# Another form of the RWKV inverse, of the head sums and of the S5 transposes, with other beat counts, in a three-layer hybrid kernel

## Chip, cores and metric

The kernel runs on one core of a Trainium2 chip. The metric is the device time of one execution in microseconds (us); less is better.

## What is computed

A sequence of 256 tokens of width 2048 passes two layers of a first block and one layer of a second, all in float32.

```python
# first block, layers l = 0, 1
shift, scale, gate = split(silu(c) @ w_ada[l] + b_ada[l], 3)
h = rms_norm(x, norm_g[l]) * (1 + scale) + shift
u, z_s, q, k, v, z_a = split(h @ w_in[l])            # 6144 columns
y_s = s5_mixer(u, ...) * silu(z_s)                   # 64 groups, 64 complex states each, then w_glu
y_a = diff_attention(rope(q), rope(k), v, ...) * silu(z_a)      # 8 heads
x = x + gate * (concat(y_s, y_a) @ w_out[l])
# second block, one layer
z_rw, z_mla, z_gate = split(rms_norm(x) @ w_in_2)
def step(state, r, w, k, v, kk, a):                  # rwkv7_scan, 16 heads of 64
    sa = state @ -kk
    state = state * w + sa (x) (kk * a) + v (x) k
    return state, state @ r
mix = (g_rw * (y_rw @ w_branch_rw) + g_mla * (y_mla @ w_branch_mla)) @ w_out_2
# then an up/conv/gelu/down feed-forward and a gated embedding, each with its norm
```

## The kernel before, in words

All activations lie transposed: channels on partitions, the 256 tokens along the free axis. The big products run as one stream through TensorE (PE). A weight tile of 128 output channels is a row of 16 (or 8, 4, 22) blocks of 128 rows; for each block `mm` multiplies a high and a low part of the float32 weights with a high and a low part of the activation, three matmuls of 256 columns. The weights come by DMA in half units of eight blocks into a ring; ScalarE (ACT) writes the high part (`hi`), VectorE (DVE) the low part (`lo`), each 128x1024. `split_ahead` and `rest` place these two beats in the order of the work.

**The order is written out beforehand.** `Timeline` makes one list of beats; each of the five engine programs walks over it and plays its own part of each beat, so every engine's queue follows this one order. Small work is woven into the stream by generators. Each step of a generator ends with a number of `yield`s, which is the number of beats until its next step. With `per=2`, as in most of `w_in`, one beat of the generators comes after two blocks (six matmuls). The counts stand in the tables `S5_PREP`, `S5_RUN`, `S5_PHASE`, `ATTENTION`, `RWKV` and `MOD_REST`, the first four with a row for each of the two layers.

**The start.** `modulation` multiplies `w_ada`, 1 MB a unit. When the last quarter of the scale is there, `gp` and four `h` (the normed activations, high part by ACT, low by DVE) follow, and then `w_in` starts. Before them stands

```python
                if parts == 3:
                    self.split_ahead(1)
                    self.rest(0)
```

which puts the first two `hi` and the first `lo` ahead of the last four `h`. The later modulation units are woven into the stream; `MOD_REST` holds the beats between the request for a unit and its matmuls, for `w_in`'s first eight tiles, for the rest of `w_in` with `w_outa`, and for the last two streams.

**S5.** 16 blocks of four groups per layer. `s5_prepare` makes the matrices of block b+1 while `s5_follow` runs block b; a block ends when the longer one has ended (`s5_phases` too in every second block). In the preparation the taps are multiplied in step 6 (PE), copied by ACT in step 7, written by GpSimd (POOL) to the DRAM scratch `scr_k`, and read back in step 8 by four DMAs into `WI`, with overlapping rows. In the run, step 0 makes the inputs `x` in bank 3, step 1 (ACT) copies them to `XT`, twice side by side, step 2 (PE) transposes `XT` and `XT` shifted by 64 columns, so that DVE has real and imaginary halves in both orders, step 3 (DVE) rotates and scans, step 4 (PE) waits for `WI` and for the scan and makes `y`.

**RWKV.** Eight pairs of heads `i` in chunks of 32 tokens; a pair is steps 0 to 14 of `rw`. Step 0 multiplies the low-rank weights `LW` (`GD2`, `GD` for the gate into bank 5, two halves for decay and `a` into banks 3 and 4, then `over` for the key norms). Its signal `d` lets ACT, DVE and again PE (`rk`, step 3) go on. Step 4 makes the score blocks, and DVE masks them. Sixteen 32x32 blocks (two heads, two token halves, four chunks) form a strictly triangular matrix whose inverse is needed. With the 16x16 blocks on the diagonal, steps 6 to 9 build the inverse `EE` by squaring; steps 10 and 11 add the corner part: `OT` times `EE` and a transposed `EE`, ACT copies, `ET` times `TO`, which DVE adds to `EE`; step 12 applies `EE` to `Q0T` (`apply`, 96 columns) and ACT copies the result to `QTT`. Step 13 makes `G` and the transition matrices, step 14 the chunk sums in banks 3 to 6 for states (64 columns) and for outputs (32 columns), which DVE takes out as `Af` and `Y` (signal `af`, which step 0 of the next pair waits for).

**`rw_seq`.** Steps c = 1 to 7 run over the chunks for all 16 heads: PE makes the carried states (`tf`) and output parts (`ty`), heads of one parity on partitions 0 to 63 and the others on 64 to 127 of one bank; DVE scales, adds, and adds the outputs to `Y`. Two beats of stream lie behind each step. DVE's queue holds `cq` and `part` work between them.

Of the kernel before, what the change touches and what calls it, by code (L numbers as in the profile page):

```python
# [26 lines left out]
for _n, _c in PARAMS:  # L27
# [4 lines left out]
    ("ident", 128), ("rot", 128), ("ones", 128), ("blk", 128), ("spare", 256), ("caus", 128), ("chk", 128),  # L32
    ("m16s", 32), ("m32i", 32), ("m16t", 32), ("m32t", 32), ("mot", 32), ("i32", 32), ("scm", 256), ("id64", 64),
# [14 lines left out]
def const_array():  # L48
# [75 lines left out]
ROOM = _c.alloc(320)  # L124
# [50 lines left out]
OT, ET, TO = (BTM + 128 * n for n in range(3))  # L175
# [99 lines left out]
def kind_of(name, n):  # L275
# [44 lines left out]
class Timeline:  # L320
# [429 lines left out]
    def run(self):  # L750
# [15 lines left out]
        for n, _ in enumerate(first):  # L766
# [323 lines left out]
def tensor_program(pe, m, tl, D):  # L1090
# [111 lines left out]
    def s5_run(l, b, i):  # L1202
# [67 lines left out]
    def rw(i, s, slot):  # L1270
# [34 lines left out]
        if s == 0:  # L1305
# [17 lines left out]
        if s == 4:  # L1323
# [3 lines left out]
            if i:  # L1327
                pe.wait_ge("rw_dve", ("af", i - 1))
# [48 lines left out]
        if s == 13:  # L1377
            pe.wait_ge("rw_act", ("a3", i))
# [3 lines left out]
        if s == 14:  # L1382
            pe.wait_ge("rw_dve", ("vm", i))
            rows(0, 64, KE, 64, VTK, 64)
            rows(256, 32, VTK, 64, MRK, 32).then_inc("rw_pe", ("e", i))

    def rw_seq(c):
# [3 lines left out]
        if c < 7:  # L1391
            for i in range(8):
                for hd, p in enumerate(rows):
                    x = pe.mm(B(3, 64 * i, 64, **p), V(BK + 512 * i + 64 * c, 64, **p), V(before + 64 * i, 64, **p), True, True)
            x.then_inc("rw_pe", ("tf", c))
        pe.wait_ge("rw_dve", ("ys", c - 1))
        for i in range(8):
            for hd, p in enumerate(rows):
                x = pe.mm(B(5, 32 * i, 32, **p), V(before + 64 * i, 64, **p), V(G + 256 * i + 32 * c, 32, **p), True, True)
# [111 lines left out]
def scalar_program(act, m, tl, D):  # L1511
# [1419 lines left out]
```

## Time and profile before

| what | value |
|---|---|
| median of three runs | 2895.5 us (2895.36 to 2900.58) |
| profiled execution, own time | 2895.5 us |
| its span | 2893.6 us |
| PE busy | 2781.8 us (96%) |
| DVE busy | 2008.9 us (69%) |
| ACT busy | 1468.2 us (51%) |
| POOL busy | 288.5 us (10%) |
| chain that ended last | PE 84%, DVE 7%, DMA 6% |

The profile is of one execution. The span runs from the first to the last instruction; the own time holds what lies around it, 1.9 us. Busy times are sums over an engine's instructions. The chain that ended last goes back from the last instruction to what released it, step by step.

### The profile page before, as it was taken

How to read it: one execution, taken by the hardware profiler on the slowest of the kernel's cores; microseconds unless marked ns; L12 is line 12 of the kernel's file. 1: busy time of each engine (PE TensorE's matmuls, PEld its weight loads, DVE VectorE, ACT ScalarE, POOL GpSimd, SP SyncE). 2: the span in 40 equal slices, each digit the busy share in tenths (PEclk: the TensorE clock that was granted, in tenths of full speed). 3: DMA queues.
4: the chain of work that ended last, by engine and by line, in shares of the span. 5: the costliest groups of instructions: out<-in, count | busy, mean ns of one | idle time of the engine just before them, and what ended most of it. 6: DMA issues, size and time to landing. Idle time of an engine off the chain costs nothing.

```text
span 2893.6 us, 64415 instructions
## 1 busy us (share of the span) xinstructions
PE 2781.8 (96%) x27664; PEld 2593.9 (90%) x27664; DVE 2008.9 (69%) x3478; ACT 1468.2 (51%) x2406; POOL 288.5 (10%) x488
## 2 busy tenths in 40 slices
PE   6899999999999999999999999999999999999987
PEld 2678788788999999999889889999999999999987
DVE  6357778687799986765556566666888547887565
ACT  3335556355566656644444435456555445555454
POOL 0012222100123221200011011100000000000000
PEclk9899999999999999999999999999999999999999
DMA  9988788885756566555444445554555555555543
GB/s 392 332 267 269 260 287 267 292 310 169 205 171 199 175 204 197 181 175 169 140 144 150 140 133 170 180 193 161 185 182 187 184 184 180 181 185 187 182 153 110
DMA packets 168236, 581.08 MB, mean 201 GB/s; under 512 B 40272, under 2 KB 40304, under 8 KB 155536
## 3 DMA queue, kind: packets, MB, share of 16 engines
q1 hardware_dynamic: 146784, 525.40, 54.2%
q0 software_dynamic: 20592, 48.26, 5.4%
q8 instruction: 218, 3.57, 0.5%
q10 hardware_dynamic: 576, 3.31, 0.3%
q14 instruction: 66, 0.54, 0.1%
HBM read 555.06 MB, written 21.76 MB: 199 GB/s over the span
## 4 chain that ended last, share of the span: by engine, by line
PE 84%; DVE 7%; DMA 6%; ACT 1%; issue 1%; SPq 1%; POOL 0%; DVEq 0%; ACTq 0%
PE acc L1011 82%; DMA arena<-in_w_ada 3%; DVE arena L979 2%; PE acc L1014 2%; DVE rounded L979 2%; DMA scr_k<-arena 1%; DMA arena<-scr_k 1%; SPq L976 1%; DVE upper L987 1%; DMA scr_u<-upper 0%; DVE arena L987 0%; ACT arena L1008 0%; DVE rounded L987 0%; DVE upper L979 0%; DMA arena<-in_w_outm 0%
## 5 line engine op out<-in xcount | busy, mean ns | idle before, releaser
L1011 PE MATMUL acc<-rounded 128*128 128x256 f32 x14592 | 1861.9, 286 | 18.6 <-issue 10.1
L1011 PEld LDWEIGHTS acc<-rounded 128*128 128x128 f32 x14592 | 1783.5, 192 | 86.2 <-issue 61.2
L1008 ACT ACTIVATE rounded<-arena 128x1024 fp32r<-128x1024 f32 (+1 forms) x862 | 875.3, 1022 | 694.5 <-PE acc L1011 583.5
L979 DVE TENSOR_TENSOR rounded<-arena,rounded 128x1024 fp32r<-128x1024 f32 (+1 forms) x830 | 983.9, 1198 | 246.7 <-ACT rounded L1008 246.1
L1011 PEld LDWEIGHTS acc<-upper_rounded,rounded 128*128 128x128 f32 x4656 | 560.8, 192 | 18.2 <-issue 9.8
L1011 PE MATMUL acc<-upper_rounded,rounded 128*128 128x256 f32 x4656 | 567.7, 284 | 2.8 <-DVE rounded L979 2.0
L1008 ACT ACTIVATE arena<-arena 128x256 f32<-128x256 f32 (+3 forms) x473 | 232.9, 515 | 170.8 <-DVE arena L979 105.4
L979 DVE TENSOR_TENSOR arena<-acc,arena 128x256 f32<-128x256 f32 (+5 forms) x270 | 113.7, 431 | 233.7 <-PE acc L1011 221.0
L979 DVE TENSOR_TENSOR arena<-arena 128x256 f32<-128x256 f32 (+5 forms) x455 | 233.3, 526 | 35.9 <-ACT arena L1008 27.5
L987 DVE SCALAR_TENSOR_TENSOR arena<-arena 128x256 f32<-128x256 f32 (+5 forms) x465 | 205.1, 446 | 27.7 <-ACT arena L1008 19.6
L1011 PE MATMUL acc<-arena 128*32 128x512 f32 (+6 forms) x1990 | 183.2, 402 | 41.7 <-DMA arena<-in_w_ada 27.6
L1008 ACT ACTIVATE arena<-acc 128x256 f32<-128x256 f32 (+3 forms) x267 | 99.2, 384 | 187.6 <-PE acc L1011 179.2
L1011 PEld LDWEIGHTS acc<-arena 128*32 128x32 f32 (+2 forms) x1990 | 69.6, 123 | 97.0 <-DMA arena<-in_w_ada 50.7
L1008 ACT ACTIVATE upper<-acc 128x128 f32<-128x128 f32 (+3 forms) x184 | 67.4, 380 | 114.2 <-PE acc L1011 82.5
L1008 ACT ACTIVATE arena<-acc,arena 128x256 f32<-128x256 f32 (+1 forms) x148 | 59.3, 428 | 103.3 <-PE acc L1011 91.2
L1011 PE MATMUL acc<-upper 32*32 32x32 f32 (+8 forms) x4384 | 101.3, 218 | 9.1 <-issue 3.3
L1011 PEld LDWEIGHTS acc<-upper 32*32 32x32 f32 (+4 forms) x4384 | 73.1, 114 | 30.0 <-issue 13.5
L976 POOL DMA_DIRECT2D arena<-scr_k x128 | 77.3, 621 | 122.5 <-DMA scr_k<-arena 121.8
L1011 PE MATMUL acc<-upper,arena 64*64 64x64 f32 (+4 forms) x490 | 63.0, 350 | 13.7 <-DMA upper<-in_w_ada 6.9
L976 POOL DMA_DIRECT2D scr_g<-arena x56 | 30.4, 545 | 440.4 <-DVE arena L990 236.6
L1014 PE MATMUL acc<-arena 128*128 128x128 f32 x416 | 71.2, 276 | 2.8 <-ACT arena L1008 2.3
L1008 ACT ACT_TABLE_LOAD x56 | 71.8, 1283 | 4.0 <-issue 3.0
(92 smaller groups left out, 1116.0 us busy)
## 6 DMA issues: line engine op xcount, KB each, us to landing
arena<-in_w_in SPq DMA_DIRECT2D x328, 512.0 KB, 4.8
arena<-in_w_ada SPq DMA_DIRECT2D x88, 1024.0 KB, 5.5
arena<-in_w_up SPq DMA_DIRECT2D x176, 512.0 KB, 3.9
arena<-in_w_down SPq DMA_DIRECT2D x88, 512.0 KB, 4.2
arena<-in_w_outa SPq DMA_DIRECT2D x32, 512.0 KB, 6.0
arena<-in_w_glu SPq DMA_DIRECT2D x32, 512.0 KB, 5.8
arena<-in_w_outm SPq DMA_DIRECT2D x32, 512.0 KB, 4.6
arena<-in_w_out SPq DMA_DIRECT2D x32, 512.0 KB, 3.8
```

Of the source, the lines that this page charges most:

```text
L976: self.e.dma_start(out, in_).then_inc(self.signals.sems[sem], 16)
L979: return self.put(self.e and self.e.tensor_tensor(o, a, b, op))
L987: return self.put(self.e and self.e.scalar_tensor_tensor(out=o, in0=a, scalar=s, in1=b, op0=o1, op1=o2))
L1008: return self.put(self.e and self.e.activation(o, a, f, scale=scale, **kw))
L1011: return self.put(self.e and self.e.matmul(o, l, r, start=start, stop=stop, skip_group_check=True))
L1014: return self.put(self.e and self.e.transpose(o, i, self.m.con("ident")))
```

## The change

- The beats `split_ahead(1)` and `rest(0)` ahead of the last four `h` are taken out; the splits follow behind them.
- The beat counts of S5, of attention and of `MOD_REST` are others.
- S5, run: ACT copies 128 columns to `XT` instead of 256. PE transposes them once, and makes the second, swapped order by two matmuls of 64 stationary columns each with the identity.
- RWKV steps 10 to 12: instead of completing `EE` and applying it once, `EE` is applied to `Q0T`, the corner part `OO` (masked by DVE in step 4 from the other scores) to the result, and `EE` again to that; DVE adds the first and the last. ACT copies 384 columns after steps 10 and 11.
- RWKV step 14: the outputs come from four matmuls over all 128 partitions with 128 columns; DVE spreads `MRK` with the chunk mask to `MRW` for it (128x512, in step 13). They lie in bank 7, and ACT copies them to `Y`.
- RWKV step 0: `kr` is waited for first and `gd` last; the two halves for `d` come first, `over` next, the gate last, with 32 rows of `GD2` instead of 64.
- `rw_seq`: the heads of the two parities go to two banks (3 and 4, 5 and 6), and DVE does its product and its sum out of them in two instructions of 64 partitions.
- The constants lose 128 columns, and `ROOM`, which nothing uses, gains them.

```diff
-S5_PREP = ((0, 0, 3, 7, 1, 5, 0, 3, 0),
-    (0, 2, 0, 4, 2, 6, 2, 2, 0))
-S5_RUN = ((1, 3, 1, 7, 1, 3, 1, 2),
-    (1, 5, 2, 6, 1, 3, 1, 1))
-S5_PHASE = ((18, 1),
+S5_PREP = ((0, 1, 3, 6, 1, 6, 1, 2, 0),
+    (1, 2, 2, 4, 3, 3, 3, 1, 0))
+S5_RUN = ((1, 3, 1, 6, 2, 3, 2, 1),
+    (1, 4, 3, 6, 2, 1, 1, 1))
+S5_PHASE = ((13, 5),
     (17, 2))
 S5_START = (6, 8)
-ATTENTION = ((1, 1, 3, 2, 3, 4, 4, 1, 2, 1, 1, 2, 5, 2, 1),
-    (1, 1, 2, 2, 1, 1, 4, 1, 5, 2, 3, 3, 3, 1, 2))
+ATTENTION = ((1, 2, 4, 2, 3, 2, 4, 1, 3, 1, 1, 2, 2, 2, 1),
+    (1, 1, 2, 1, 2, 2, 4, 1, 5, 2, 2, 3, 3, 2, 1))
 RWKV = (1, 3, 3, 6, 3, 4, 2, 2, 2, 1, 2, 2, 2, 4, 1)
-MOD_REST = (2, 3, 2)
+MOD_REST = (2, 2, 2)
...
-                if parts == 3:
-                    self.split_ahead(1)
-                    self.rest(0)
...
             pe.wait_ge("s5_act", ("xt", l, b))
+            pe.tr(B(3, 256, 128), V(XT, 128))
             for h in range(2):
-                x = pe.tr(B(3, 256 + 128 * h, 128), V(XT + 64 * h, 128))
+                x = pe.mm(B(3, 384, 128, p0=64 * h, np_=64), V(XT + 64 - 64 * h, 64), con("ident"), True, True)
...
+            pe.wait_ge("rw_dve", "kr")
+            pe.mm(B(3, 0, 256), V(LW, 128, np_=64), V(LO, 256, np_=64), True, True)
+            pe.mm(B(4, 0, 256), V(LW, 128, p0=64, np_=64), V(LO, 256, p0=64, np_=64), True, True).then_inc("rw_pe", ("d", i))
+            over(6, 0, KNR + 2 * i).then_inc("rw_pe", ("kk", i))
             pe.wait_ge("rw_dve", "gd")
-            pe.mm(B(5, 0, 256), V(LW + 256, 128, np_=64), V(GD2, 256, np_=64), True, False)
-            pe.mm(B(4, 0, 256), V(LW, 128, p0=64, np_=64), V(LO, 256, p0=64, np_=64), True, True)
-            pe.mm(B(3, 0, 256), V(LW, 128, np_=64), V(LO, 256, np_=64), True, True).then_inc("rw_pe", ("d", i))
-            pe.mm(B(5, 0, 256), V(LW + 128, 128), V(GD, 256), False, True).then_inc("rw_pe", ("g", i))
-            pe.wait_ge("rw_dve", "kr")
-            over(6, 0, KNR + 2 * i).then_inc("rw_pe", ("kk", i))
+            pe.mm(B(5, 0, 256), V(LW + 128, 128), V(GD, 256), True, False)
+            pe.mm(B(5, 0, 256), V(LW + 256, 128, np_=32), V(GD2, 256, np_=32), False, True).then_inc("rw_pe", ("g", i))
...
         if s == 10:
             pe.wait_ge("rw_dve", ("e3", i))
-            four(3, OT, EE)
-            for u, p in chunks():
-                x = pe.mm(B(4, 32 * u, 32, **p), V(EE + 32 * u, 32, **p), V(CON + CCOL["i32"], 32, **p), True, True)
-            x.then_inc("rw_pe", ("a1", i))
+            apply(3, EE, 32, Q0T).then_inc("rw_pe", ("a1", i))
         if s == 11:
             pe.wait_ge("rw_act", ("a1", i))
-            four(5, ET, TO).then_inc("rw_pe", ("a2", i))
+            apply(5, OO, 32, QTT).then_inc("rw_pe", ("a2", i))
         if s == 12:
-            pe.wait_ge("rw_dve", ("a2", i))
+            pe.wait_ge("rw_act", ("a2", i))
             apply(3, EE, 32, Q0T).then_inc("rw_pe", ("a3", i))
...
-            rows(0, 64, KE, 64, VTK, 64)
-            rows(256, 32, VTK, 64, MRK, 32).then_inc("rw_pe", ("e", i))
+            rows(0, 64, KE, 64, VTK, 64).then_inc("rw_pe", ("e", i))
+            for u, (hd, hf) in enumerate(U4):
+                x = pe.mm(B(7, 128 * hf, 128, p0=64 * hd, np_=64), V(VTK + 64 * u, 64), V(MRW + 128 * u, 128), True, True)
+            x.then_inc("rw_pe", ("y", i))
...
-                    x = pe.mm(B(3, 64 * i, 64, **p), V(BK + 512 * i + 64 * c, 64, **p), V(before + 64 * i, 64, **p), True, True)
+                    x = pe.mm(B(3 + hd, 64 * i, 64, **p), V(BK + 512 * i + 64 * c, 64, **p), V(before + 64 * i, 64, **p), True, True)
...
-            dve.tt(V(D2, 8, 64), B(3, 0, 8, 64), V(PL + c, (8, 8), (0, 64)), MUL)
+            for hd, p in enumerate(rows):
+                dve.tt(V(D2, 8, 64, **p), B(3 + hd, 0, 8, 64, **p), V(PL + c, (8, 8), (0, 64), **p), MUL)
...
-        y = V(Y + 32 * c, (256, 8), (1, 32))
-        dve.tt(y, y, B(5, 0, 8, 32), ADD).then_inc("rw_dve", ("ys", c))
+        for hd, p in enumerate(rows):
+            y = V(Y + 32 * c, (256, 8), (1, 32), **p)
+            x = dve.tt(y, y, B(5 + hd, 0, 8, 32, **p), ADD)
+        x.then_inc("rw_dve", ("ys", c))
```

## Rows read from the trace of the kernel before

**Rows 1.** The page, part 1: busy us of each engine, share, instructions.

```profile
PE 2781.8 (96%) x27664; PEld 2593.9 (90%) x27664; DVE 2008.9 (69%) x3478; ACT 1468.2 (51%) x2406; POOL 288.5 (10%) x488
```

**Rows 2.** PE's waits, 1290 to 1740 us: us in total, times, longest.

```profile
PE acc L1011 <- DVE upper L987: 3.2, 4, 1.3
PE acc L1011 <- DVE arena L990: 2.1, 7, 0.3
PE acc L1011 <- DVE upper L984: 1.7, 1, 1.7
```

**Rows 3.** Timeline at the start of the stream: start, us, instruction, count, [idle before].

```profile
103.85 4.86 PE L1011 MATMUL acc<-rounded 128*128 128x256 f32 x24 [0.75 <-DVE rounded L979]
...
107.09 2.95 ACT L1008 ACTIVATE rounded<-arena 128x1024 fp32r<-128x1024 f32 x3
...
107.62 4.62 DVE L979 TENSOR_TENSOR rounded<-arena,rounded 128x1024 fp32r<-128x1024 f32 x4
...
108.89 1.45 PE L1011 MATMUL acc<-rounded 128*128 128x256 f32 x10 [0.18 <-DVE rounded L979]
```

**Rows 4.** Timeline of PE, 360 to 372 us (S5 and stream).

```profile
363.38 0.64 PE L1011 MATMUL acc<-arena,upper 128*32 128x128 f32 x16
...
369.39 0.27 PE L1014 MATMUL acc<-arena 128*128 128x128 f32 x1
369.60 0.43 PE L1011 MATMUL acc<-arena 128*32 128x128 f32 x8
369.95 2.30 PE L1011 MATMUL acc<-rounded 128*128 128x256 f32 x17
```

**Rows 5.** Timeline of PE, 1737 to 1742 us (`over` in `rw_post`).

```profile
1738.01 1.09 PE L1011 MATMUL acc<-arena,upper 128*64 128x128 f32 x16 [0.83 <-DVE arena L979]
```

**Rows 6.** Timeline, 330 to 387 us: taps written, read, and two uses.

```profile
340.68 0.65 PE L1011 MATMUL acc<-arena,upper 128*32 128x128 f32 x16 [1.90 <-DMA arena<-scr_k]
...
370.66 0.55 POOL L976 DMA_DIRECT2D scr_k<-arena  x1 [4.90 <-ACT arena L1008]
375.74 2.43 POOL L976 DMA_DIRECT2D arena<-scr_k  x4 [4.53 <-DMA scr_k<-arena]
...
386.19 0.65 PE L1011 MATMUL acc<-arena,upper 128*32 128x128 f32 x16
```

**Rows 7.** The tile view of `scr_k`, 375.7 to 378.6 us: the four reads.

```profile
DMA to landing us min/median/max: 6.1/6.7/8.1
```

**Rows 8.** Timeline of PE, 1510 to 1536 us: steps 10 to 14 of one pair.

```profile
1517.93 0.45 PE L1011 MATMUL acc<-upper 32*32 32x32 f32 x32
...
1518.61 1.69 PE L1011 MATMUL acc<-rounded 128*128 128x256 f32 x12
...
1522.23 0.87 PE L1011 MATMUL acc<-upper 32*32 32x96 f32 x32
1523.03 1.69 PE L1011 MATMUL acc<-rounded 128*128 128x256 f32 x12
...
1529.03 0.89 PE L1011 MATMUL acc<-upper 32*64 32x64 f32 x64
```

**Rows 9.** Timeline, 1709 to 1725 us, DVE and PE (`rw_seq`).

```profile
1711.40 0.69 DVE L979 TENSOR_TENSOR upper<-acc,upper 128x512 f32<-128x512 f32 x1 [0.18 <-PE acc L1011]
...
1721.07 0.68 DVE L979 TENSOR_TENSOR upper<-acc,upper 128x512 f32<-128x512 f32 x1
...
1722.96 1.12 PE L1011 MATMUL acc<-upper 64*64 64x32 f32 x32 [1.84 <-DVE arena L979]
```

**Rows 10.** Windows: length, busy us of PE, PEld, DVE, ACT, POOL, clock, DMA share, GB/s.

```profile
1698.00:1722.90 24.90, 22.44 (x462) 21.12 (x461) 18.58 (x34) 5.15 (x8) 4.03 (x6) 1.00 0.45 144
130.00:700.00 570.00, 547.55 (x4661) 463.06 (x4659) 419.80 (x771) 291.26 (x534) 99.86 (x168) 0.99 0.82 272
```

**Rows 11.** PE's groups by shape, 1290 to 1740 us: busy us, mean ns, idle.

```profile
L1011 PE MATMUL acc<-upper,arena 64*64 64x64 f32 x192 | 6.9, 221 | 0.7 <-DVE upper L990 0.7
L1011 PE MATMUL acc<-arena 64*32 64x64 f32 x512 | 6.9, 224 | 0.0
```

More of the change, by code:

```diff
@@ L70, in const_array @@
     put("m16s", (i < j) & (i // 16 == j // 16))
+    put("mo", (i < j) & (i // 16 != j // 16))
     put("m32i", i <= j)
@@ L123 @@
 CON = _c.alloc(NCON)
-ROOM = _c.alloc(320)
+ROOM = _c.alloc(448)
 COS = _c.alloc(256)
@@ L174 @@
 CQ, CQH = Q0T, BTM + 768
-OT, ET, TO = (BTM + 128 * n for n in range(3))
+MRW = BTM
 MPR, MPT, MSM, MNM = TMPS + 1024, TMPS + 1408, TMPS + 1792, TMPS + 1800
@@ L1327, in rw @@
             if i:
-                pe.wait_ge("rw_dve", ("af", i - 1))
+                pe.wait_ge("rw_act", ("y", i - 1))
                 if i == 3:
@@ L1444, in cq_norm @@
                 pe.wait_ge("sum_dve", ("ev", tl.out_of["w_in2", 0, 28 + n].o))
-            pe.wait_ge("rw_dve", ("af", 2))
+            pe.wait_ge("rw_act", ("y", 2))
             for a, at in enumerate((RS, RS2)):
@@ L1656, in s5_run @@
     def s5_run(l, b, i):
-        if i == 1:
-            act.wait_ge("s5_pe", ("x", l, b))
-            act.act(V(XT, 2, 128), B(3, 0, (0, 2), (1, 128)), ACT.Copy).then_inc("s5_act", ("xt", l, b))
-        for at, pe_key, to, src, key in ((5, "y", YT, 128, "yt"), (7, "yu", U8 + 128 * b, 0, "y")):
+        for at, pe_key, to, src, key in ((1, "x", XT, 0, "xt"), (5, "y", YT, 128, "yt"), (7, "yu", U8 + 128 * b, 0, "y")):
             if i == at:
@@ L1749, in rw @@
             act.wait_ge("rw_pe", ("a1", i))
-            act.act(V(TO, 128), B(3, 0, 128), ACT.Copy)
-            act.act(V(ET, 128), B(4, 0, 128), ACT.Copy).then_inc("rw_act", ("a1", i))
-        if s == 12:
-            act.wait_ge("rw_pe", ("a3", i))
-            act.act(V(QTT, 4, 96), B(3, 0, (128, 4), (1, 96)), ACT.Copy).then_inc("rw_act", ("a3", i))
+            act.act(V(QTT, 4, 96), B(3, 0, (128, 4), (1, 96)), ACT.Copy).then_inc("rw_act", ("a1", i))
+        if s == 11:
+            act.wait_ge("rw_pe", ("a2", i))
+            act.act(V(Q0T, 4, 96), B(5, 0, (128, 4), (1, 96)), ACT.Copy).then_inc("rw_act", ("a2", i))
+        if s == 14:
+            act.wait_ge("rw_pe", ("y", i))
+            act.act(V(Y + 256 * i, 256), B(7, 0, 256), ACT.Copy).then_inc("rw_act", ("y", i))
     def rw_post(i, s):
@@ L2259, in rw_zero @@
         dve.ts(V(GP, 16), V(PAR + PCOL["post_mix"], 16), 0.5, None, MUL)
-        dve.memset(V(GD2, 256, p0=32, np_=32), 0.0)
         dve.memset(V(KPZ, 256, np_=64), 0.0).then_inc("rw_dve", "init")
@@ L2313, in rw @@
             dve.tt(f4(DD), quad(3, 0), mask("m16s"), MUL)
+            dve.tt(f4(OO), quad(3, 0), mask("mo"), MUL)
             dve.tt(f4(MBT, 96), quad(3, 32), mask("m32i"), MUL).then_inc("rw_dve", ("m3", i))
@@ L2327, in rw @@
             dve.tt(V(EE, 128), V(EE, 128), B(5, 0, 128), ADD).then_inc("rw_dve", (e, i))
-        if s == 11:
-            dve.wait_ge("rw_pe", ("a2", i))
-            dve.tt(V(EE, 128), V(EE, 128), B(5, 0, 128), ADD).then_inc("rw_dve", ("a2", i))
+        if s == 12:
+            dve.wait_ge("rw_pe", ("a3", i))
+            dve.tt(V(QTT, 4, 96), V(QTT, 4, 96), B(3, 0, (128, 4), (1, 96)), ADD).then_inc("rw_dve", ("a3", i))
         if s == 13:
@@ L2335, in rw @@
             dve.tt(V(KE, 4, 64), V(KTT, 4, 64), B(7, 32, (128, 4), (1, 64)), ADD)
+            dve.settle()
+            dve.tt(V(MRW, 4, 4, 32), V(MRK, (32, 4), (0, 4), (1, 32)), V(CON + CCOL["ch4"], (0, 4), (1, 4), (0, 32)), MUL)
             dve.wait_ge("rw_pe", ("gf", i))
@@ L2341, in rw @@
             dve.wait_ge("rw_pe", ("e", i))
-            dve.tt(V(Af, 2, 4, 64), B(3, 0, (128, 2), (512, 4), (1, 64)), V(PL + 8 * i, (4, 2), (1, 4), (0, 64)), MUL)
-            dve.copy(V(Y + 256 * i, 2, 4, 32), B(3, 256, (128, 2), (512, 4), (1, 32))).then_inc("rw_dve", ("af", i))
+            dve.tt(V(Af, 2, 4, 64), B(3, 0, (128, 2), (512, 4), (1, 64)), V(PL + 8 * i, (4, 2), (1, 4), (0, 64)), MUL).then_inc("rw_dve", ("af", i))
     def rw_seq(c):
@@ L2347, in rw_seq @@
         if c == 1:
+            dve.wait_ge("rw_act", ("y", 7))
             dve.wait_ge("rw_dve", ("af", 7))
             dve.copy(V(STS[0], 8, 64), V(AR, (512, 8), (1, 64))).then_inc("rw_dve", ("st", 0), ("ys", 0))
+        rows = [dict(p0=64 * hd, np_=64) for hd in range(2)]
         if c < 7:
             dve.wait_ge("rw_pe", ("tf", c))
-            dve.tt(V(D2, 8, 64), B(3, 0, 8, 64), V(PL + c, (8, 8), (0, 64)), MUL)
+            for hd, p in enumerate(rows):
+                dve.tt(V(D2, 8, 64, **p), B(3 + hd, 0, 8, 64, **p), V(PL + c, (8, 8), (0, 64), **p), MUL)
             dve.settle()
@@ L2666, in extras @@
         b, g = extra_places(i)
[L2667 removed]
+        free = (("rw_act", ("y", 7)), ("rw_dve", ("ys", 7)), ("rw_dve", ("yo", 0)), ("rw_dve", ("yo", 1)))[i]
         pool.wait_ge(*free)
```

11 lines of the change are left out of this document (4 added, 7 removed).

## The prediction

> **What bounds the kernel now.** I read the page first, then the waits and the timeline of TensorE (PE) stage by stage. PE is busy 2781.8 of 2893.6 us [rows 1]. The reader is to see there that any PE work added in line costs its own time, and that an added wait has little idle time to hide in. So the sum below is one of PE work added or taken, and of PE waits made or ended. Three stretches matter: the start of the weight stream near 103 us, the S5 work of two layers, and the RWKV stage of 1340 to 1740 us. In the last, the waits of PE that this change touches are short and regular: seven of 0.3 us for a VectorE (DVE) copy, four for `rk`, one for `gd` [rows 2].
>
> **1. Start of the stream.** Before, `hi(0)`, `hi(1)` and `lo(0)` come ahead of the last four tiles of `h`, and PE works on the first half unit from 103.85 and on the second from 108.89 [rows 3]. With those beats removed, ScalarE (ACT) and DVE do `gp` and the four `h` first. These end today at about 107.1 (ACT) and 107.6 (DVE), where the next copies begin; they would begin 1.0 us earlier, being behind one DVE copy less. Then `hi(0)` takes 1.0 (2.95 for three) and `lo(0)` 1.2: PE has its first low half at 108.35. Its first 24 matmuls took 4.86 us; at the pace that the stream has later (12 in 1.69 [rows 8]) they would take 3.3. The second half unit so starts between 111.6 and 113.2, against 108.89: a loss of 2.7 to 4.3, and I take **+3.8**. Nothing returns it: the stream then goes at PE's pace.
>
> **2. S5, 32 blocks.** One transpose stays; the other becomes two calls of 128 rows by 64 columns, which are four instructions, as an fp32 matmul is two here. ACT copies 128 columns instead of 256, which is off the path in all but a few blocks and is costed at nothing: its cover is the three beats to the next step, and uncovered it would give back 0.1 us a block. The shape 128*64 took 1.09 us for 16 instructions, 0.065 each [rows 5]. A burst between other shapes also pays for the turn: 8 instructions of 128*32 start 0.21 after a transpose begins, of which about 0.1 is the transpose, and the stream goes on 0.35 after them; 16 take 0.64 against 0.43 for 8 (0.026 each), so about 0.13 of the 0.35 is the turn out and 0.1 goes in [rows 4]. Four instructions cost 0.26 + 0.13 + 0.10, less the transpose of 0.1: 0.39. Without any turn it is 0.16, without overlap of the two column tiles 0.6. Over 32 blocks: 5 to 20, I take **+12.3**.
>
> **3. S5 beat counts of layer 0.** The taps go from ACT's copy (`s5_prep` step 7) through a DMA to `scr_k`, four DMAs back, and are waited for by `s5_run` step 4 of the next block. Before, step 7 stands 16 beats into its block (0+0+3+7+1+5+0), blocks last 20 and 21 beats in turn, and the use stands at beat 12 (1+3+1+7): 16 or 17 beats between them. After, step 7 stands at 18, a block of layer 0 lasts 21 beats (the preparation is 20 long) and the use is at 11: 14 beats. A beat is 1.1 us (a block took 22.8, from 363.38 to 386.19) [rows 4, 6]. The copy no longer waits for its own matmuls in that beat, which returns some 0.6, so the chain loses 2.2 us. It has them seldom: the write at 370.66 led to reads at 375.74, the last landed 8.1 after its issue at 377.5, and the use was at 386.19, a margin of 0.6; another use waited 1.90 [rows 6, 7]. Of the 14 blocks used between 213 and 518 us, two waited already (2.2 more each), two had a margin of 0.6 (1.6 each), one of 2.0 (0.2), the others 2.3 to 6.0 (nothing). That is **+7.8**, with 0 if the DMAs land as fast as in other places and 11 if they bunch. In layer 1 the step moves from 19 beats ahead to 16 or 17, which is ample. The S5 tail moves 2 beats later in layer 0 (it ended 10 blocks of matmuls ahead of the drain) and loses nothing. `MOD_REST` at 2 moves every `w_ada` matmul by one beat, but the next load is issued when the last one is used, so the distance of issue to use stays: nothing. The `ATTENTION` counts leave at least 5 beats from sums to transpose: nothing.
>
> **4. RWKV, 8 head pairs.** A burst of 16 calls of 32x32 costs 0.34 in the middle of others (32 in 0.68, from 1517.93 to 1518.61) and an `apply` of 16 calls with 96 columns costs 0.80 (1522.23 to 1523.03) [rows 8]. Steps 10 to 12 were 0.68 + 0.38 + 0.80 and become three times 0.80: +0.54. In step 14, 16 of 32 small calls go (half of 0.89) and four calls of 128*64 come, eight instructions at 0.065 to, with no overlap, 0.13 [rows 5]; the order takes one head's two calls first, so between: 0.75, and 0.2 for the turns. Together +0.5. In step 0 the shapes turn once more and `GD2` no longer lies beside another row half: +0.2. Sum 1.24 by 8 = **+9.9**, ends 6 and 14.
> Given back: PE's wait for the Y copy goes (2.1 over seven), as `af` now follows a shorter burst and no DVE copy stands behind it; `d` comes two instructions earlier, which takes 0.4 off each of four waits for `rk`; and `gd` is waited for behind `d` and `kk`, 0.5 once [rows 2]: **-4.2**. The ACT and DVE copies of 384 columns in steps 10 to 12, about 0.5 each, lie under two beats of stream (1.6), and the DVE product for `MRW` (512 columns, 0.69 [rows 9]) under the four beats behind step 13; uncovered they would cost 0.1 and 0.7 a pair.
>
> **5. `rw_seq`.** DVE's product over 128 partitions becomes two over 64, each as long as the whole one, 0.69 [rows 9], in steps 1 to 6; the small sums double too (0.34 in flow, seven times): 6 to 7 us more of DVE in a stretch where it is busy 18.6 of 24.9 us [rows 10]. Through step 3 the slack holds it. From step 4 on `cq`, `part` and `lo` fill DVE's queue: one product starts at 1711.40 and, two steps on, at 1721.07, which is 4.8 a step, and PE waits 1.84 at 1722.96 already [rows 9]. With 0.7 lost ahead of step 4 and 0.95 in each of three steps, PE resumes 3.5 later: **+3.5**, ends 2 and 5. The two banks gain PE nothing: one bank held both heads, yet 192 instructions of 64 columns took 6.9 us, 36 ns each with their edges, about half of the 0.065 that twice the columns took on 128 rows, so the bank costs them nothing that a row shows [rows 5, 11].
> The Trainium skill, "TensorEngine Tiling (Array Packing)", Gotcha 1, says that different row tiles cannot access the same PSUM bank simultaneously. By it the two heads took turns, and two banks would make `rw_seq` shorter; the rival below prices that from rows. No row here shows turns taken, but none settles it.
>
> **Sum** against the profiled execution, whose own time is 2895.5, equal to the median: 3.8 + 12.3 + 7.8 + 9.9 - 4.2 + 3.5 = +33.1, so **2929 us**.
>
> **The rivals.**
> A. The taps are not late (the DMA bunches in other beats): +25, 2921. For it: most margins are above 2.3. Against: two waits today.
> B. The heads in `rw_seq` run side by side only in two banks: the scores, which do write a bank for each head, took 13.5 ns an instruction (512 in 6.9), against 36 [rows 11]. PE would then save up to 0.9 a step, but DVE's 25.6 us for a stretch of 24.9 is the floor: +0.7 in place of +3.5, 2926.
> C. The new matmuls overlap badly: S5 at 20, step 14 and taps at their high ends (+7.7, +4, +3): +48, 2944.
> D. Not slower. Mechanism: PE's waits of 130 to 700 us are all made by the placement of steps, and the new counts end them. PE idled 570.0 - 547.5 = 22.5 us there [rows 10]. With S5 at its low end (5) and no late taps the rest is 3.8 + 5 + 9.9 - 4.2 + 3.5 = +18, so it decides from 18 of 22.5 us won back; all won: -4.5, 2891. Against it: the largest of those waits are for `w_ada`, whose distance does not change.
> E. The edits in RWKV hide (waits of PE swallow them): +20, 2915. Against: the waits named there are 7.0 us in all [rows 2], and the sum takes 4.2 of them already.
>
> **How the numbers follow.** Forecast 0.47, A 0.20, B 0.08, C 0.10, E 0.08, D 0.04, and 0.03 for a sum that ends near nothing. A, B and E reach down to 2915, and with S5 at its low end 2908; C gives 2944. The range is 2908 to 2944. A change of 0.2% (5.8 us) is what a measurement of this kernel can tell: slower 0.93, same 0.03, faster 0.04.
>
> **What would show it.** The second half unit starts near 112.7. A burst of four 128*64 instructions follows one transpose in each S5 block, and PE's waits for the DMA from `scr_k` are 8 to 12 us in total instead of 2.6. Steps 10 to 12 show three bursts of 32x96 of 0.80. No waits for L990 of 0.3 are left. In `rw_seq`, DVE is nearly full and PE waits over 4 us in all. The forecast fails if PE's waits between 130 and 700 shrink, or if the 128*64 bursts cost under 0.2.

## The result and the profile after

The changed kernel takes 2945.7 us (median of four runs, 2942.7 to 2948.3) against 2896.0 (2895.4 to 2900.6) for the one before: ratio 1.0166, 95% interval 1.0146 to 1.0184, +48 us (42 to 53). Measured again beside other kernels it was 1.0160 (1.0143 to 1.0178), +46.4. The forecast was 2929, +33, with a range up to 2944. Below, a ratio is turned into us by a time before of 2898; the run-to-run spread makes each such number uncertain by 3 to 5 us. The profiled execution took 2932.6 us, span 2930.8, at the low end; a second one had a span of 2939.7. Page, part 1, of the first, to be laid beside [rows 1]:

```profile
PE 2810.9 (96%) x27312; PEld 2604.6 (89%) x27312; DVE 2023.4 (69%) x3490; ACT 1467.3 (50%) x2406; POOL 289.9 (10%) x488
```

TensorE (PE) has 29.1 us more work, though some of that is the same work at a lower clock. I compared the traces by the start of every n-th block of the weight stream, which both kernels issue in the same order. The second trace of the changed kernel is 5.4 us behind before at the first block, 3.6 at block 480, 18.9 at 768 (end of layer 0's `w_in`), 17.1 at 1152, 32.3 at 1920 (end of layer 1's `w_in`), 30.2 at 2784, 36.7 at 3360 (RWKV pairs) and 46.7 at 3456 (`rw_seq` and its tail). Nothing is lost afterwards. In the first trace the same points are 5.3, 1.8, 14.7, 15.5, 27.6, 25.5, 32.3 and 37.8.

Timeline of the start of the stream, after, against [rows 3]:

```profile
106.40 3.89 ACT L1005 ACTIVATE rounded<-arena 128x1024 fp32r<-128x1024 f32 x4
...
107.48 4.63 DVE L976 TENSOR_TENSOR rounded<-arena,rounded 128x1024 fp32r<-128x1024 f32 x4 [0.46 <-ACT rounded L1005]
107.59 0.77 PE L1008 MATMUL acc<-rounded 128*128 128x256 f32 x2 [4.80 <-ACT rounded L1005]
108.76 6.81 PE L1008 MATMUL acc<-rounded 128*128 128x256 f32 x34 [0.40 <-DVE rounded L976]
```

The low part of the first half unit comes at 108.7, near the forecast (108.35), and PE then runs on without a stop. Before, PE had done 24 matmuls by that time. The second half unit starts at 113.6, 5.3 us later than before: the forecast had 112.7, because it took a pace between the slow one of the start and the fast one of later, and the granted clock was 0.50 from 107 to 114 us.

Line numbers differ between the kernels: PE's matmuls are L1011 and its transposes L1014 before, L1008 and L1011 after, and a kernel made from either has the numbers of that one or close to them.

PE's waits, 500 to 740 us and 740 to 1300 us, after (us in total, times, longest):

```profile
PE acc L1011 <- ACT arena L1005: 6.6, 1, 6.6
PE acc L1008 <- DMA arena<-in_w_ada: 4.1, 2, 2.7
...
PE acc L1011 <- ACT arena L1005: 3.9, 2, 2.8
```

This is the surprise. L1011 is a transpose here, and `acc <- ACT arena` means that it waits for something ScalarE (ACT) writes. Before, the largest wait of this kind was 1.5 us. These are the transposes at the end of attention (step 13). The waits for the taps, where the forecast put the loss, are 3.4 us in 130 to 500 against the 2.6 of before. The timeline of all engines shows what the longest of the three hangs on:

```profile
496.06 0.54 POOL L973 DMA_DIRECT2D scr_k<-arena  x1 [9.50 <-ACT arena L1005]
...
505.37 2.41 POOL L973 DMA_DIRECT2D arena<-scr_k  x4 [8.23 <-DMA scr_k<-arena]
507.85 0.22 POOL L980 TENSOR_SCALAR arena<-arena 128x2 f32<-128x2 f32 x1
508.15 0.72 POOL L976 TENSOR_TENSOR arena<-arena 128x2 f32<-128x2 f32 x1
...
508.91 0.62 ACT L1005 ACTIVATE arena<-acc,arena 128x128 f32<-128x128 f32 x2 [6.74 <-POOL arena L976]
...
509.59 0.69 PE L1011 MATMUL acc<-arena 128*128 128x128 f32 x2 [6.55 <-ACT arena L1005]
509.93 1.63 PE L1008 MATMUL acc<-rounded 128*128 128x256 f32 x6
```

Read it from the transposes (509.59) upward. PE waits for ACT's scaling of the attention output; ACT waits for two scalars that GpSimd (POOL) makes (`att` step 11); and these stand in POOL's queue behind the four reads of the taps, which wait 8.23 us for the write of the taps to land. The scalars have nothing to do with the taps. In the kernel before, the same head's scalars had a place of their own (POOL, timeline):

```profile
488.96 2.41 POOL L976 DMA_DIRECT2D arena<-scr_k  x4 [5.92 <-DMA scr_k<-arena]
...
497.84 0.50 POOL L983 TENSOR_SCALAR arena<-arena 128x2 f32<-128x2 f32 x1 [5.88 <-ACT arena L1008]
```

The order written out beforehand says where else. In layer 0 the new attention row leaves 8 blocks of stream between scalars and transposes instead of 14; in layer 1 it leaves 12, as before. With the new S5 rows the reads fall 0 blocks ahead of the scalars of head 7 in layer 0 and of head 3 in layer 1, and 4 blocks ahead of those of layer 1's head 5. PE waits at exactly these three: 6.55 at 509.59, 2.77 at 924.34, 1.15 at 988.78 (6.52, 3.89 and 1.54 in the second trace).

The same collision, in a milder form, already stood in the kernel before. In its order the reads fall 0 blocks ahead of the scalars at head 1 of layer 0, with 14 blocks from there to the transposes (timelines of POOL and PE, before):

```profile
281.99 2.40 POOL L976 DMA_DIRECT2D arena<-scr_k  x4 [5.83 <-DMA scr_k<-arena]
284.46 0.37 POOL L983 TENSOR_SCALAR arena<-arena 128x2 f32<-128x2 f32 x1
...
286.45 0.44 PE L1014 MATMUL acc<-arena 128*128 128x128 f32 x2 [1.52 <-ACT arena L1008]
```

So the trace that the forecast was made from shows the mechanism, at a price of 1.5 us.

Such a pause costs more than its length. Windows of the second trace (length; busy us of PE, PEld, DVE, ACT, POOL; granted clock; DMA share; GB/s):

```profile
500.00:510.00 10.00, 6.21 (x54) 4.70 (x52) 5.48 (x8) 5.31 (x12) 1.81 (x4) 0.95 0.85 281
510.00:520.00 10.00, 7.27 (x36) 6.63 (x37) 3.79 (x10) 2.38 (x5) 2.49 (x5) 0.53 0.43 130
520.00:530.00 10.00, 10.00 (x98) 8.33 (x97) 8.32 (x17) 5.77 (x12) 0.56 (x1) 1.00 0.55 170
...
920.00:930.00 10.00, 6.11 (x42) 5.24 (x39) 6.27 (x10) 5.96 (x11) 8.13 (x12) 0.78 0.59 154
```

The pause ends at 512.7, and in the ten us that hold its end the granted clock is 0.53 of full speed, near the lower of its two levels (1.2 of 2.4 GHz). The six stream matmuls right behind the pause take 1.63 us in both traces, and 0.97 at full clock. From block 700 to block 730, which hold the wait, the stream falls 7.5 us further behind in the first trace and 8.5 in the second, for waits of 6.55 and 6.52.

The RWKV pair looks as forecast (timeline of PE, against [rows 8]):

```profile
1543.67 0.87 PE L1008 MATMUL acc<-upper 32*32 32x96 f32 x32
1544.47 1.70 PE L1008 MATMUL acc<-rounded 128*128 128x256 f32 x12
...
1555.32 1.08 PE L1008 MATMUL acc<-upper 32*64 32x64 f32 x40
1556.33 0.97 PE L1008 MATMUL acc<-rounded 128*128 128x256 f32 x6
```

Three bursts of 0.80 (the first is shown; the others start at 1546.10 and 1548.52), and step 14 takes 1.01 against 0.82.

### The profile page after: what moved, and what is told of

Its sections match the earlier page's. It is cut to its first block, busy times and chain, and to the rows that moved or that the text cites. A ratio compares the mean times of both kernels' runs of the same rounds, so it can differ in the third digit from the quotient of the medians.

```text
span 2930.8 us, 63709 instructions
## 1 busy us (share of the span) xinstructions
PE 2810.9 (96%) x27312; PEld 2604.6 (89%) x27312; DVE 2023.4 (69%) x3490; ACT 1467.3 (50%) x2406; POOL 289.9 (10%) x488
## 4 chain that ended last, share of the span: by engine, by line
PE 85%; DVE 6%; DMA 5%; ACT 1%; issue 1%; POOL 0%; SPq 0%; DVEq 0%; ACTq 0%
PE acc L1008 84%; DMA arena<-in_w_ada 2%; DVE arena L976 2%; PE acc L1011 2%; DVE rounded L976 1%; DMA scr_k<-arena 1%; DMA arena<-scr_k 1%; DVE upper L984 1%; DMA upper<-in_w_ada 1%; ACT arena L1005 0%; DVE rounded L984 0%; DVE upper L976 0%; DVE arena L984 0%; POOL arena L973 0%; ACT L1005 0%
## 5 line engine op out<-in xcount | busy, mean ns | idle before, releaser
L1008 PE MATMUL acc<-rounded 128*128 128x256 f32 x14592 | 1876.9, 287 | 20.9 <-issue 9.3
L1008 PEld LDWEIGHTS acc<-rounded 128*128 128x128 f32 x14592 | 1787.9, 192 | 101.9 <-issue 78.9
L1008 PEld LDWEIGHTS acc<-upper_rounded,rounded 128*128 128x128 f32 x4656 | 562.5, 192 | 17.4 <-issue 14.8
L1008 PE MATMUL acc<-upper_rounded,rounded 128*128 128x256 f32 x4656 | 569.0, 284 | 1.6 <-DVE rounded L976 0.7
L976 DVE TENSOR_TENSOR arena<-arena 128x256 f32<-128x256 f32 (+4 forms) x455 | 234.6, 526 | 36.9 <-ACT arena L1005 28.7
L1008 PE MATMUL acc<-arena 128*32 128x512 f32 (+8 forms) x2118 | 196.4, 396 | 38.0 <-DMA arena<-in_w_ada 20.5
L1008 PEld LDWEIGHTS acc<-arena 128*32 128x32 f32 (+3 forms) x2118 | 73.5, 122 | 98.1 <-DMA arena<-in_w_ada 43.3
L1008 PE MATMUL acc<-upper 32*32 32x32 f32 (+9 forms) x4192 | 112.2, 226 | 8.4 <-issue 6.8
L1008 PEld LDWEIGHTS acc<-upper 32*32 32x32 f32 (+7 forms) x4192 | 77.5, 114 | 30.5 <-issue 12.8
L1011 PE MATMUL acc<-arena 128*128 128x128 f32 x384 | 70.2, 278 | 11.6 <-ACT arena L1005 11.4
L1008 PE MATMUL acc<-upper,arena 64*64 64x64 f32 (+4 forms) x490 | 64.6, 357 | 17.2 <-DMA upper<-in_w_ada 8.0
```

Of the source, the lines that this page charges most:

```text
L976: return self.put(self.e and self.e.tensor_tensor(o, a, b, op))
L1008: return self.put(self.e and self.e.matmul(o, l, r, start=start, stop=stop, skip_group_check=True))
L1011: return self.put(self.e and self.e.transpose(o, i, self.m.con("ident")))
```

## The experiments

Each kernel was timed in five rounds beside the kernel before. Kernels of one group ran on the same chip.

**First group: the tables, the rest, and two parts of the rest.** `tables_only` has the new `S5_PREP`, `S5_RUN`, `S5_PHASE`, `ATTENTION` and `MOD_REST` and nothing else; `all_but_tables` is the opposite; `rwkv_only` has all hunks of `rw` and `rw_seq`, and `s5_order_only` has the S5 order with the single copy to `XT`:

```diff
+            pe.tr(B(3, 256, 128), V(XT, 128))
...
+                x = pe.mm(B(3, 384, 128, p0=64 * h, np_=64), V(XT + 64 - 64 * h, 64), con("ident"), True, True)
```

> The kernel before with only the new beat tables (S5, attention, MOD_REST). Theory: the tables cause the part of the loss that the forecast did not name. With the preparation's steps 7 and 8 two beats apart instead of three, GpSimd waits in its queue for the landing of the tap write, attention's scalars stand behind that wait, and TensorE then waits for ScalarE at the attention transposes (6.55 us at 509.6, 2.77 at 924.3 in the changed kernel). Expected: 8 to 20 us slower than before, 2904 to 2916, and an uneven time from run to run (more than 5 us between lowest and highest), with TensorE waits for ScalarE of over 2 us near 510 or 924. Rival: the tables cost what the forecast took for the taps, about 8 us, as waits on the read of scr_k, or nothing (2896) and with the spread of before; then the excess and the spread come with the other parts.

1.0040 (1.0025 to 1.0055), +11.6. Its trace has the attention waits at the same three places: 4.91 at 499.19, 2.74 at 909.52, 1.98 at 974.34. Those for the taps are 2.1 us in all. The theory's place is confirmed; its spread is not, 4.9 us between lowest and highest of five runs.

> The changed kernel with the beat tables of before. Theory: the other parts cost start 4 to 5, S5 transposes 11.5 (0.36 a block, 32 blocks), RWKV pairs 6, rw_seq 4 to 5.5: together 25 to 28, so 2921 to 2924, with a spread as small as before's. Rival: the spread and the excess are in these parts (their waits or a clock fall), and the time stays at 2935 or more.

1.0075 (1.0060 to 1.0091), +21.7, a little under the theory, and no attention wait over 1.4.

> The kernel before with only the S5 transposes changed: one transpose, the swapped order by four 128x64 matmul instructions, and the single copy to XT. Theory: 0.36 us a block in the line of TensorE, 32 blocks, +11.5, 2907; TensorE busy up by about 11. Rival A: waits behind it swallow part, +5 or less. Rival B: the later steps slip onto waits, +15 or more.

1.0022 (1.0012 to 1.0032), +6.4: rival A. The matmuls are there: 128 instructions of 128*64 in 14.1 us, 0.44 a block. PE's idle time between 105 and 1300 us is 22.8 us against 29.0 before, so waits took in 6. The profiled run is the slowest of the twelve: its stream is 7.0 behind at block 1920, where the edited work ends, and 16 at the end, so the time of that one execution says less than the median.

> The kernel before with only the RWKV edits: step 0, steps 10 to 12, step 14 and rw_seq. Theory: pairs +6 (1.2 a pair in step 0, 10 to 12 and 14, less 2.1 for the copies of Y and less one wait on gd, and nothing for rk) and rw_seq +5: +11, 2906 to 2908, with the waits on rk at 0.6 to 1.3 as before. Rival: rw_seq alone is hidden and the sum is +6; or the half clock behind rw_seq is the larger part and the sum is +15.

1.0052 (1.0036 to 1.0069), +15. In its trace the pairs lose nothing up to block 3072, 5.0 go between blocks 3072 and 3360, still in the pairs, and 8.5 between 3360 and 3456, in `rw_seq` and its tail. That is the second rival: the part in `rw_seq` is the larger one.

**Second group: is the whole more than its parts, and is POOL's queue the cause?** `scalars_first` changes only the order in which POOL's program walks the beats:

```diff
+    beats = list(tl.beats)
+    for l, h in ((0, 7), (1, 3), (1, 5)):
+        i = beats.index(("att", l, h, 11))
+        j = max(k for k in range(i) if beats[k][0] == "s5_prep" and beats[k][3] == 8)
+        beats.insert(i, beats.pop(j))
```

`s5_prep` step 8 exists on no other engine, so the edit moves the four reads behind the two scalars at three places, and nothing else. `without_s5_order` is the changed kernel less the S5 order.

> The changed kernel once more, in the same company as the next three. The parts measured so far add to less than the whole: the tables alone gave +11.6 and all but the tables +21.7, 33 together, against +48 for the whole. Theory: the parts add on top of each other because the same attention waits grow when other parts have pushed the steps; the whole stays at +45 to +50. Rival: the first number was high by chance of its chip, and the whole is +33 to +40 here.

1.0160 (1.0143 to 1.0178), +46.4: the whole is more than its parts.

> The changed kernel, with the four reads of the taps moved behind attention's scalars in GpSimd's queue at the three places where these two meet (layer 0 head 7, layer 1 heads 3 and 5); everything else keeps its place. Theory: TensorE's waits for ScalarE at 509.6, 924.3 and 988.8 (6.55, 2.77, 1.15 us) go, and the half clock behind the first: 9 to 13 us faster than the changed kernel. Rival: the scalars wait for ScalarE anyway, or the reads come too late for their own use, and the gain is under 4.

1.0118 (1.0100 to 1.0136), +34.2, so **12.2 us come back** from moving twelve DMA issues. Its timeline around the same head:

```profile
502.44 0.22 POOL L980 TENSOR_SCALAR arena<-arena 128x2 f32<-128x2 f32 x1 [2.23 <-ACT arena L1005]
...
505.14 0.63 ACT L1005 ACTIVATE arena<-acc,arena 128x128 f32<-128x128 f32 x2
...
505.95 0.38 PE L1011 MATMUL acc<-arena 128*128 128x128 f32 x2
...
508.20 2.48 POOL L973 DMA_DIRECT2D arena<-scr_k  x4 [4.73 <-DMA scr_k<-arena]
```

Its window of 510 to 520 us, to be laid beside the one above that has a clock of 0.53:

```profile
510.00:520.00 10.00, 8.60 (x81) 7.20 (x81) 8.86 (x18) 4.62 (x10) 1.82 (x4) 1.00 0.94 300
```

The scalars run at 502.44, PE doesn't wait, and the reads go out at 508.20, as late as their write lets them in either order (508.50 in the second trace of the changed kernel). From block 700 to 730 the stream falls 0.4 us behind instead of 8.5, and at block 1920 it is 19.8 behind instead of 32.3. This shows the cause of these 12 us. Not all that the pause held is won: PE now waits 1.4 us for these same taps at 515.78, a wait that the longer one had covered.

> The kernel before with only the two banks in rw_seq and DVE's two halves of 64 partitions for each product and sum. Theory: in the trace of the kernel with all RWKV edits the stream lost 8.5 us between 1696 and 1760, with DVE waits of up to 4.2 us and a granted clock of 0.90; so +7 to +9 alone (2906 to 2908), and the matmul bursts keep their length of about 1.0 us. Rival: the loss needs the other RWKV edits (DVE's queue delayed by the product for MRW), and alone it is +3.5, as forecast.

1.0030 (1.0020 to 1.0040), +8.7: it needs no other edit. DVE's groups from 1698 to 1735 us in this kernel, then in the kernel before:

```profile
L979 DVE TENSOR_TENSOR upper<-acc,upper 64x512 f32<-64x512 f32 x12 | 8.3, 688 | 1.8 <-PE acc L1011 1.6
L979 DVE TENSOR_TENSOR arena<-arena,acc 64x256 f32<-64x256 f32 x14 | 5.9, 419 | 1.5 <-PE acc L1011 1.2
```

```profile
L979 DVE TENSOR_TENSOR upper<-acc,upper 128x512 f32<-128x512 f32 x6 | 4.1, 688 | 4.0 <-PE acc L1011 4.0
L979 DVE TENSOR_TENSOR arena<-arena,acc 128x256 f32<-128x256 f32 x7 | 2.9, 414 | 0.5 <-PE acc L1011 0.5
```

A half costs what the whole cost (688 ns and 688, 419 and 414), so DVE has 7.2 us more (4.2 in the products, 3.0 in the sums); the forecast said 6 to 7. PE's timeline shows what that does:

```profile
1720.21 1.18 PE L1011 MATMUL acc<-upper,arena 64*64 64x64 f32 x32 [2.08 <-DVE upper L979]
1721.19 1.85 PE L1011 MATMUL acc<-upper 64*64 64x32 f32 x32
1722.98 2.93 PE L1011 MATMUL acc<-rounded 128*128 128x256 f32 x12
...
1728.09 1.92 PE L1011 MATMUL acc<-upper 64*64 64x32 f32 x32 [2.18 <-DVE arena L979]
...
1731.38 5.53 PE L1011 MATMUL acc<-arena 128*128 128x256 f32 x16
```

After the waits the clock falls (the windows 1720 to 1730 and 1730 to 1740 have 0.56 and 0.76; before 1.00 and 0.83). Twelve stream matmuls take 2.93 us instead of 1.70, and the 16 of the next step 5.53 instead of 3.80. Of before:

```profile
1719.42 1.70 PE L1011 MATMUL acc<-rounded 128*128 128x256 f32 x12
...
1724.82 3.80 PE L1011 MATMUL acc<-arena 128*128 128x256 f32 x16
```

PE's waits in `rw_seq` are 0.37, 0.57, 2.08 and 2.18, together 5.2, against 1.84 before: 3.4 more, where the forecast had 3.5. The five bursts from 1721.19 to 1736.74, waits left out, take 5.2 more than the same five before. The two make 8.6, against the 8.7 measured. The forecast had the waits and not the clock.

> The changed kernel with S5's two transposes and the double copy as before; all else changed. The S5 order alone cost +6.4 where the line of TensorE holds 11.5 more. Theory: in the changed kernel there is no slack left to swallow it, so taking it out gives back 10 to 14 us. Rival: it gives back 6, as it cost alone, and the excess of the whole over the parts lies elsewhere.

1.0111 (1.0094 to 1.0129), +32.2: the theory. The S5 order is worth 14.2 in the changed kernel and 6.4 alone.

**Third group: the parts not yet seen, and a version that might beat both.** `start_only` takes out the three lines at `parts == 3`; `rwkv_pairs_only` is `rwkv_only` less `rw_seq`; `old_attention` is the changed kernel with the attention rows of before; `before_scalars_first` is the kernel before with the edit of `scalars_first` at layer 0, heads 1 and 6.

> The kernel before with only the first two high parts and the first low part of the weights taken out from ahead of the last four tiles of h. Theory: the stream starts 5 us later, but TensorE's waits for w_ada and the taps behind it shrink, since the transfers had longer; the trace of the kernel with all but the tables kept 3.4 of its first 6 us at block 480. So +1 to +4, 2900 to 2902. Rival: nothing is given back, +5. Other rival: all is given back, 0.

1.0018 (1.0007 to 1.0028), +5.2. Its trace is 6.1 behind at the first block and 2.6 at block 480; the time does not tell a small return from none.

> The kernel before with the RWKV edits of the eight pairs (step 0, steps 10 to 12, step 14) and rw_seq as before. Theory: all RWKV edits gave +14 to +15 and rw_seq alone +8.7, so the pairs cost +5 to +6, as forecast (+5.7 net). Rival: the parts of RWKV do not add, and the pairs cost 0 to 2 or over 9.

1.0005 (0.9993 to 1.0018), +1.4: within the rival, though the interval, -2 to +5 us, reaches the low end of the theory. In its trace the stream falls 5.4 behind over the pairs (blocks 2784 to 3360); but in the nine traces whose RWKV is that of before or has `rw_seq` alone changed it falls 1.0 to 7.0 behind there too, for no edit of theirs. A cost of some 4 us is not excluded. With `rw_seq` that is 10, at the lower end of the interval of `rwkv_only` (10 to 20).

> The changed kernel with the attention row of before; the S5 rows and MOD_REST stay new. In layer 0, head 7, the reads of the taps then stand 12 blocks ahead of the scalars instead of 0, and the transposes 14 blocks behind the scalars instead of 8. In layer 1 nothing changes. Theory: the wait of 6.5 at 509 and the half clock behind it go, those at 924 and 988 stay: 7 to 10 us faster than the changed kernel. Rival: head 3 of layer 0, whose scalars now stand 0 blocks behind the reads, waits instead, and the gain is under 3.

1.0147 (1.0131 to 1.0162), +42.6, only 4 back: between theory and rival. The wait at 512 is gone and those of layer 1 stay (3.22 and 1.08), as the theory said. But layer 0's waits on the taps rose to 5.1 us, those on `w_ada` in the same stretch to 6.4, and the stream is 7.4 behind at block 480, where it was 3.6. Moving the scalars away from one collision moved other things into waits on DMAs.

> The kernel before with the reads of the taps moved behind attention's scalars at the two places where these are close (layer 0, heads 1 and 6). Theory: the wait of 1.52 at 286.45 goes; the 14 blocks between scalars and transposes cover the rest: -1 to -2. Rival: no difference, since waits for w_ada take up what is won.

0.9994 (0.9980 to 1.0008): not to be told from no change. No kernel of this study is shown to beat the one before.

**Fourth group: which table, and where is the excess?**

> The kernel before with only the new S5 rows. In layer 0 head 3's scalars stand 0 blocks behind the reads of the taps but 14 ahead of the transposes; in layer 1 head 3's 0 and 12, head 5's 4 and 12. Theory: the S5 rows carry the waits of layer 1 (2.7 and 2.0 in the trace of all tables) and more waits for the taps in layer 0: +5 to +8. Rival: the S5 rows alone are free and the loss needs the attention row: under +2.

1.0055 (1.0036 to 1.0075), +16, above the theory and more than all tables together; its seven runs lie 20 us apart, so the interval is 10 to 22 us. Its trace waits for the taps 4.8 us before 500 and 2.5 after, together 7.3 against 2.6 before: with the S5 rows alone the taps are late, nearly as forecast (8 to 12). It waits for the attention transposes 1.95, 1.44 and 1.48.

> The kernel before with only the new attention rows. Theory: scalars and reads do not meet at a short distance (head 1 stands 0 blocks behind the reads and 8 ahead of the transposes, where it had 14): that one wait grows from 1.5 to 3 to 5, so +2 to +4. Rival: nothing, the w_ada waits behind it take it up.

1.0027 (1.0018 to 1.0036), +7.8. The wait named grew as said, from 1.5 to 4.0, in PE's waits from 280 to 290 us:

```profile
PE acc L1014 <- ACT arena L1008: 4.0, 1, 4.0
```

The granted clock is 0.83 in the ten us around it, and the sum is twice what the theory gave. It is again head 1, whose transposes now stand 8 blocks behind the scalars instead of 14. The two tables cost 24 singly and 11.6 together with `MOD_REST`. What one row costs depends on the others.

> The kernel before with all new tables and the S5 order. Alone they gave +11.6 and +6.4. Theory: the excess of the whole over its parts (13) lies for the larger part between these two, because the tables leave no wait in which the order's 11.5 us of matmuls could disappear: +22 to +26. Rival: the two add, +18, and the excess needs the later start or RWKV.

1.0096 (1.0083 to 1.0110), +27.8, above both: 18 if they added. It is a little above the theory too (22 to 26). The attention waits are 6.30, 3.89 and 1.54, as in the whole kernel.

> The changed kernel with the S5 rows of before; attention's rows and MOD_REST stay new. Layer 1 is then as before (no scalars within 12 blocks of the reads), in layer 0 head 1 stands at 0 and 8 blocks. Theory: most of the tables' part and of the excess comes back: 17 to 24 us faster than the changed kernel, 2921 to 2928. Rival: the attention rows or MOD_REST hold half of it, and the gain is 8 to 14.

1.0128 (1.0113 to 1.0142), +37.1, so 9 come back: the rival's case. Head 1's wait of layer 0 is 3.6 here.

**Fifth group: both mends, and the mend beside the tables alone.**

> The changed kernel with both mends: attention's scalars ahead of the reads of the taps at the three places, and S5's two transposes as before. Alone they gave back 12 (scalars) and 14 (order). Theory: the order's excess over the 6.4 that it costs in the kernel before comes through those three waits, so beside the first mend the second is worth 6 to 8: 2924 to 2927. Rival: the two give back independently, 26 together: 2917 to 2920.

1.0086 (1.0071 to 1.0100), +24.9. Beside the first mend the S5 order is worth 9.3, between theory and rival: apart the two gave back 26.4, together 21.5. Some 5 us are shared.

> The kernel before with all new tables (+11.6 alone), and the scalars ahead of the reads at the same three places. Theory: the tables' loss is these waits and the half clock behind them: 0 to +3, 2898 to 2901. Rival: the taps and the other waits of the tables hold half of it, +5 to +8.

1.0033 (1.0022 to 1.0044), +9.6: above even the rival. The theory is refuted: most of what the tables cost alone is not these waits. By the ratios the mend gives 2 here, with an uncertainty of 5; in the trace the stream is 5.5 behind at block 1920, where that of `tables_only` was 13.4. A wait of 1.8 for ACT stands new in layer 1, and those for the taps are 4.0 where they were 2.1.

## Why the prediction was wrong

The mechanism "more PE work in line, more waits" was right and the direction too. The time lies above the range. By the steps of the prediction:

| step | forecast | alone |
|---|---|---|
| 1. start | +3.8 | +5.2 |
| 2. S5 order | +12.3 | +6.4 |
| 3. tables (as late taps) | +7.8 | +11.6 |
| 4. RWKV pairs, net | +5.7 | +1.4 |
| 5. `rw_seq` | +3.5 | +8.7 |
| sum | +33.1 | +33.3 |
| the whole, measured | | +46.4 |

That the two sums agree is luck: the terms are off by +1.4, -5.9, +3.8, -4.3 and +5.2, and these cancel.

**The step that failed is step 3**, in two sentences. One, "the `ATTENTION` counts leave at least 5 beats from sums to transpose: nothing", looked at the distance in the order alone. The scalars in between are made by POOL, whose queue holds the reads of the taps, and those wait for a write to land. I named who waits for the taps (S5's step 4) and not what is queued behind their reads. The other put the tables' loss on late taps: the waits for them came to 3.4 us in the changed kernel and 2.1 with the tables alone, not 8 to 12 (with the S5 rows alone 7.3, so the working fitted those rows, and not the rows beside the new attention row). With the three groups of reads moved behind the scalars the whole is +34.2, inside the range. The step failed in the whole kernel above all: beside the tables alone the same mend gave back 2.

**Step 5** was mis-sized: the doubled products came as costed, and PE's added waits too (3.4 for 3.5), but the half clock behind them, 5.2 us, was not in the sum. [Rows 10] had shown a clock of 1.00 in that stretch; with the waits it was 0.56 from 1720 to 1730.

**Step 2**: the instructions cost 0.44 a block, less one transpose of 0.1, near the 0.39 taken (which over 32 blocks is 12.5, not 12.3). The error was to let all of it reach the end. In the kernel before, waits swallowed nearly half. In the changed kernel the order is worth 14.2, the whole of the forecast 12.3 and 2 more.

**Step 4**: the bursts are as costed in steps 0 and 10 to 12 (+0.2 and +0.54 a pair). Step 14 rose by 0.19 a pair, not 0.5, so the bursts come to 7.6 and not 9.9. PE's waits for the `Y` copy ended (2.1), and that for `gd` fell from 1.7 to 0.5; the four waits for `rk` did not shrink (3.2 us, as before). By these rows the net is some 4. Alone the pairs measured 1.4, with an interval of -2 to +5, so how far off the term of 5.7 was is not settled.

**Step 1** held in kind: 5.2 against 3.8, with the interval 2 to 8, and 5.3 in the trace at the second half unit, above the 4.3 that it had as its upper end.

**Rival A** (taps not late) was half right: in the changed kernel the taps were hardly late, and the tables still cost time. **Rival B** was false: the 32 instructions of 64x64 and the 32 of 64x32 behind them take 0.98 and 1.00 us from start to next start with one bank (1702.98, 1703.96, 1704.96 before) and with two (1735.67, 1736.65, 1737.66 in the second trace of the changed kernel). The Trainium skill, "TensorEngine Tiling (Array Packing)", Gotcha 1, has it that different row tiles can't access one bank at the same time; by that two banks would have made them shorter, and these bursts do not bear it out. **Rival C** gave +48, 2944, all but the number measured, and by another mechanism: S5 at 20 us, step 14 at its high end and taps later still. None of that came (S5's bursts 0.44 a block, step 14 +0.19 a pair, waits for the taps 3.4), so the agreement is chance. **D** and **E** did not come.

**What stays open.** The parts without the tables add up (6.4 + 8.7 + 5.2 + 1.4 = 21.7, measured 21.7), more exactly than their intervals of about 3 us each way give a right to expect. With the tables there are 13 us more than the sum (uncertain by some 8, from the intervals); 10 of them are there with the tables and the S5 order alone (27.8 against 18.0). That moving three groups of reads takes 12.2 of the whole away is shown. What the tables cost by themselves, +9.6 with the mend in, has no shown cause. Why the same mend gives less beside the tables alone is only argued: there the other waits of PE, for `w_ada` and the taps, may take in what is won. New waits of 1.6 and 1.8 us in its trace, and the 5 us that the S5 order shares with the mend, speak for it, but the intervals of these small differences are as wide as they are. The share of `MOD_REST` was not run by itself.

## What to carry to other kernels

When a step is moved in a fixed order, follow it on every queue it is played on, and ask what stands behind its waiting instruction there, even when the two have no data in common: a DMA that waits for another's landing holds up any small operation behind it. Look for a small case of it in the trace you already have: here it was a wait of 1.5 us. Put the operation with the tight reader first; the waiting one went out no later here, at the head that was looked at, because its own write had not landed yet. A cost found for one edit alone holds only with the slack that is there: edits that were cheap one by one are not cheap once another has used the slack, so add a term for that, and price a long wait of PE together with the half clock behind it, from a row of the same trace where that was seen.

## What the hardware showed that was not expected

- The landing of the same small write (240 columns by 128 partitions) varies: it took 9.3 us from its issue at 496.06 until the wait for it ended, and 2.8 from its issue at 474.26, in the same kernel and layer. The DMA engines were busy 0.87 of the one stretch and 0.67 of the other; whether that makes the difference was not tested.
- A pause of PE of 6.5 us ended in ten us (510 to 520) at a granted clock of 0.53, one of 3.9 us lay in ten us at 0.78, and in `rw_seq_only` waits of 2.1 and 2.2 us lay in and beside ten us at 0.56.
- DVE took as long for 64 partitions as for 128 (688 ns for 512 columns, both).
